# Eight blocks of a feed-forward layer in three rounded products, their low halves from an accumulating DMA

## The reference, cut to what matters

```python
h = _rmsnorm(x, norm_g[layer, 1]) * (1.0 + scale_f) + shift_f
x = x + gate_f * (jnp.square(jax.nn.relu(h @ w_fc1[layer])) @ w_fc2[layer])
```

## Time and profile before

| | |
|---|---|
| runs | 1172.93, 1177.98, 1179.79 us; median 1177.98 |
| the profiled execution | span 1171.0 us from its first to its last instruction; its time with what lies around the span is not given apart, and the runs lie 1.9 to 8.8 us above the span |
| busy share of the span | PE 95%, PEld 85%, DVE 70%, ACT 48%, POOL 4% |
| chain of work that ended last | PE 78%, DVE 10%, DMA 5%, ACT 5% |
| `fc2_0` in the trace | 306.7 to 443.3 us |
| granted clock of PE over the span | 0.985 of full speed |

### The profile page before, as it was taken

One profiled execution on the slowest core, in us unless ns is written; L12 is line 12 of the kernel. 1 busy time (PEld: TensorE's weight loads), 2 busy tenths in 40 slices (PEclk: granted clock), 3 DMA queues, 4 the chain that ended last, 5 costly groups with the idle time before them and its releaser, 6 DMA issues.

```text
span 1171.0 us, 22089 instructions
## 1 busy us (share of the span) xinstructions
PE 1112.6 (95%) x9466; PEld 995.9 (85%) x9466; DVE 816.0 (70%) x1390; ACT 557.7 (48%) x876; POOL 44.6 (4%) x71
## 2 busy tenths in 40 slices
PE   6899898999999997879999999999999999999998
PEld 4778686988888885469999999999988899988898
DVE  1599466877578674875666654478899966659955
ACT  3224633445111124554555543356568846467944
POOL 0010001000000000000000000000000000042000
PEclk8999999999999998999999999989989999999999
DMA  9887688899848957865355555525433345343342
GB/s 369 356 280 269 250 323 315 305 339 328 335 182 258 342 186 165 323 245 184 140 184 182 183 189 185 187 81 180 145 109 114 130 153 177 131 153 117 108 145 72
DMA packets 38290, 246.46 MB, mean 210 GB/s; under 512 B 4400, under 2 KB 5584, under 8 KB 9648
## 3 DMA queue, kind: packets, MB, share of 16 engines
q1 hardware_dynamic: 29072, 182.36, 45.7%
q0 software_dynamic: 6240, 43.94, 10.0%
q10 hardware_dynamic: 2880, 18.74, 3.9%
HBM read 225.24 MB, written 19.79 MB: 209 GB/s over the span
## 4 chain that ended last, share of the span: by engine, by line
PE 78%; DVE 10%; DMA 5%; ACT 5%; issue 2%; SPq 0%; ACTq 0%; DVEq 0%
PE ps L1452 16%; PE ps L1454 15%; PE ps L1456 15%; PE ps L1459 10%; PE ps L1555 4%; DMA ca_dram<-more 2%; PE ps L1648 1%; PE ps L1528 1%; PE ps L2083 1%; PE ps L1601 1%; PE ps L1539 1%; PE ps L1534 1%; DMA more<-in_ada_w 1%; DVE ring_rounded L2229 1%; DMA ada_more<-in_ada_w 1%
## 5 line engine op out<-in xcount | busy, mean ns | idle before, releaser
L1452 PE MATMUL ps<-sq_rounded,w_high_rounded 128*128 128x256 f32 x1184 | 341.6, 288 | 2.5 <-DVE mixT_rounded L2236 1.3
L1456 PE MATMUL ps<-sq_rounded,ring_rounded 128*128 128x256 f32 x1184 | 336.2, 284 | 0.0
L2229 DVE TENSOR_TENSOR ring_rounded<-ring,w_high_rounded 128x1024 fp32r<-128x1024 f32 x220 | 260.6, 1226 | 92.1 <-ACT w_high_rounded L844 91.8
L1454 PE MATMUL ps<-hT_rounded,w_high_rounded 128*128 128x256 f32 x992 | 282.1, 284 | 0.0
L844 ACT ACTIVATE w_high_rounded<-ring 128x1024 fp32r<-128x1024 f32 x220 | 219.8, 1049 | 67.0 <-PE ps L1456 66.3
L1452 PEld LDWEIGHTS ps<-sq_rounded,w_high_rounded 128*128 128x128 f32 x1184 | 228.5, 193 | 11.0 <-issue 6.7
L1456 PEld LDWEIGHTS ps<-sq_rounded,ring_rounded 128*128 128x128 f32 x1184 | 228.6, 193 | 0.0
L1454 PEld LDWEIGHTS ps<-hT_rounded,w_high_rounded 128*128 128x128 f32 x992 | 191.8, 193 | 0.1
L1452 PE MATMUL ps<-more_rounded,w_high_rounded 128*128 128x256 f32 x448 | 127.4, 284 | 0.4 <-issue 0.3
L1456 PE MATMUL ps<-more_rounded,ring_rounded 128*128 128x256 f32 x448 | 126.8, 283 | 0.0
L1459 PE MATMUL ps<-big,ring 128*128 128x256 f32 x544 | 121.0, 381 | 0.0
(11 more groups left out here) (426 smaller groups left out, 1640.3 us busy)
## 6 DMA issues: line engine op xcount, KB each, us to landing
ring<-in_blocks SPq DMA_DIRECT2D x139, 1024.0 KB, 4.9
ada_w<-in_ada_w POOLq DMA_DIRECT2D x27, 1024.0 KB, 7.7
ada_more<-in_ada_w POOLq DMA_DIRECT2D x13, 1024.0 KB, 7.6
we_dram<-we_t ACTq DMA_DIRECT2D x8, 1024.0 KB, 8.3
ca_dram<-more ACTq DMA_DIRECT2D x8, 1024.0 KB, 11.9
ring<-we_dram SPq DMA_DIRECT2D x8, 1024.0 KB, 5.5
ring<-ca_dram SPq DMA_DIRECT2D x8, 1024.0 KB, 6.8
big<-in_ada_w SPq DMA_DIRECT2D x4, 1024.0 KB, 10.9
```

The lines of the kernel that those rows point to most:

```text
L1452: nc.tensor.matmul(out, high[:, k, columns], x_high, start=start, stop=False, skip_group_check=True)
L1454: nc.tensor.matmul(out, high[:, k, columns], x_low, start=False, stop=False, skip_group_check=True)
L1456: last = nc.tensor.matmul(out, low[:, k, columns], x_high, start=False, stop=stop, skip_group_check=True)
L2229: nc.vector.tensor_tensor(rounded(w), w, w_high[:, c % 2, ks], ALU.subtract)\
```

## The change

Blocks k = 0 and 1 of each unit of `fc2_0`, eight of the 16, become split blocks. Blocks k = 2 and 3 stay plain. In the first unit the plain ones go first (order 2, 3, 0, 1), in the other units the split ones go first. In the order of the phase, blocks 0 and 1 are plain, 2 to 5 split, 6 and 7 plain, 8 and 9 split, 10 and 11 plain, 12 and 13 split, 14 and 15 plain.

The low half of these blocks' weights is made by no engine: ACT writes the high half to `w_high` and the negated rounded block over the block in the ring, and POOL then issues a DMA that reads the block from memory a second time and adds it onto the ring's slot. PE waits for that DMA once at the start of the block. ACT rounds the activations `hid` 0 to 15 into `sq` and `hT`, DVE makes their low parts in place, both before anything else of the phase on these two queues. The roundings of blocks are put between ACT's copies and stores. Since `w_high` is now in use, `near` 0 and 1 are loaded later, by ACT instead of SP, after its third square of the norm. Some semaphores are merged.

```diff
-    phase("fc2_0", [("fc2_0", k, n) for n in range(4) for k in range(4)])
+    phase("fc2_0", [("fc2_0", k, n) for n in range(4) for k in FC2_ORDER[n]])
...
+FC2_ORDER = ((2, 3, 0, 1), (0, 1, 2, 3), (0, 1, 2, 3), (0, 1, 2, 3))
+FC2_ROUND_BEHIND = {3: 4, 4: 5, 5: 6, 7: 8}
+FC2_SPLIT = tuple(4 * n + i for n in range(4) for i in range(4) if FC2_ORDER[n][i] < 2)
+LOW_BY_DMA = tuple(("fc2_0", j) for j in FC2_SPLIT)
...
+        def hid0_high(t, count):
+            return (sq if t < DT else hT)[:, t % DT:t % DT + count]
...
@@ sync
-                if b in NEAR_AT:
-                    load_near(NEAR_AT.index(b))
@@ gpsimd
+            for b in low_by_dma:
+                pool.wait_ge(w_high_ready, 2 * split_place[b] + 2)
+                pool.dma_start(rounded(ring[:, b % RING]).rearrange("p a b -> p (a b)"), dram["blocks"][laid_out[b]],
+                               accum_op=ALU.add).then_inc(w_low_dma[split_place[b] % 2], 16)
@@ scalar, round_to
+                    if b in low_by_dma:
+                        nc.scalar.activation(w_high[:, c % 2], ring[:, b % RING], ACT.Copy).then_inc(w_high_ready, 1)
+                        nc.scalar.activation(rounded(ring[:, b % RING]), ring[:, b % RING], ACT.Copy, scale=-1.0)\
+                            .then_inc(w_high_ready, 1)
...
+            def load_near(n):
+                act.wait_ge(blocks_done, first_block["fc2_0"] + FC2_SPLIT[n - 2] + 1)
+                for j in range(L):
+                    act.dma_start(s5_near[n][GC * j:GC * j + GC], ...
@@ scalar, behind the last unit of fc1_0
+            for t in range(8):
+                act.wait_ge(hid_ready, t + 1)
+                round_tiles(hid0_high(2 * t, 2), hid[:, 2 * t:2 * t + 2])
+            round_to(first_block["fc2_0"] + FC2_SPLIT[1] + 1)
             store_kernels(1)
             store_outputs(2)
             for m in range(3, 8):
...
                 copy_weights(m, (0, 1, 2, 3))
                 store_weights(m)
+                if m == 3:
+                    round_to(first_block["fc2_0"] + FC2_SPLIT[2] + 1)
                 store_kernels(m - 1)
                 store_outputs(m)
+                if m in FC2_ROUND_BEHIND:
+                    round_to(first_block["fc2_0"] + FC2_SPLIT[FC2_ROUND_BEHIND[m] - 1] + 1)
             store_kernels(7)
             act.wait_ge(k_stored, 16 * 4)
...
-            norm_stats(2, 2)
+            log_and_exp()
+            act.wait_ge(blocks_done, first_block["fc2_0"] + FC2_SPLIT[-2] + 1)
+            for p in range(3):
+                square(2, 2, p)
+            load_near(0)
+            load_near(1)
+            square(2, 2, 3)
+            norm_rstd(2)
@@ tensor, block_products
+                    if split and b in low_by_dma:
+                        if waited == 0:
+                            pe.wait_ge(w_high_ready, 2 * split_place[b] + 1)
+                            pe.wait_ge(w_low_dma[split_place[b] % 2], 16 * ((split_low[b] + 1) // 2))
+                            waited = 1
@@ vector
             s5_outputs(2)
+            for t in range(8):
+                lower_tiles("fc2_0", t, hid[:, 2 * t:2 * t + 2], hid0_high(2 * t, 2))
             gate_f = lambda k: mod(0, GATE_F, k)
```

More of the change, by code:

```diff
@@ L219, in split_plan @@
     starts = sorted((b, name) for name, b in first_block.items())
[L220 removed]
+    counts = {"vector": 0, "dma": 0}
     for i, (start, name) in enumerate(starts):
@@ L223, in split_plan @@
         for b in range(start, end) if name in SPLIT_LO else ():
-            if b - start not in {"w_in": W_IN_SPLIT, "w_out": W_OUT_SPLIT}.get(name, range(end - start)):
+            if b - start not in {"w_in": W_IN_SPLIT, "w_out": W_OUT_SPLIT, "fc2_0": FC2_SPLIT}.get(name, range(end - start)):
                 continue
@@ L229, in split_plan @@
             low[b] = counts[SPLIT_LO[name]]
-    return order, place, low
+    by_dma = [first_block[name] + j for name, j in LOW_BY_DMA]
+    return order, place, low, by_dma
 def program(nc, dram, out):
     plan, first_block = weight_plan()
-    split_order, split_place, split_low = split_plan(plan, first_block)
+    split_order, split_place, split_low, low_by_dma = split_plan(plan, first_block)
     laid_out = {b: i for i, b in enumerate(from_inputs(plan))}
-    NEAR_AT = (first_block["fc2_0"] + 10, first_block["fc2_0"] + 11)
     ctx = ExitStack()
@@ L341, in program @@
         w_low_vector = sem("w_low_vector")
+        w_low_dma = [sem(f"w_low_dma{i}") for i in range(2)]
         a_high = sem("a_high")
@@ L841, in round_to @@
                         act.wait_ge(blocks_done, split_order[c - 2] + 1 if c >= 2 else TOGETHER)
-                    for half in range(2):
+                    if b in low_by_dma:
+                        nc.scalar.activation(w_high[:, c % 2], ring[:, b % RING], ACT.Copy).then_inc(w_high_ready, 1)
+                        nc.scalar.activation(rounded(ring[:, b % RING]), ring[:, b % RING], ACT.Copy, scale=-1.0)\
+                            .then_inc(w_high_ready, 1)
+                    for half in range(2) if b not in low_by_dma else ():
                         ks = slice(4 * half, 4 * half + 4)
@@ L1443, in block_products @@
                 for k, out, columns, x, start, stop in places:
-                    if split and k // 4 == waited:
+                    if split and b in low_by_dma:
[3 more added lines that the diff above has]
+                            waited = 1
+                    elif split and k // 4 == waited:
                         pe.wait_ge(w_low_vector, 2 * split_low[b] - 1 + waited)
@@ L1500, in project_tokens, with project_deep @@
                 last.then_inc(blocks_done, 1)
-            def project_deep(phase, n, kblocks, x, arrived=None, after=None):
+            def project_deep(phase, n, kblocks, tile, arrived=None, after=None, order=range(4)):
                 ps = pair(start_unit(phase, n))
-                for kb in range(kblocks):
-                    block_products(phase, n * kblocks + kb,
+                for j, kb in enumerate(order):
+                    block_products(phase, n * kblocks + j,
                                    (lambda k: arrived(kb * KB + k)) if n == 0 and arrived else None,
-                                   [(k, ps[:, i], slice(P * i, P * i + P), at_tile(x, kb * KB + k),
-                                     kb == 0 and k == 0 and i == 0, kb == kblocks - 1 and k == KB - 1)
+                                   [(k, ps[:, i], slice(P * i, P * i + P), tile(kb * KB + k),
+                                     j == 0 and k == 0 and i == 0, j == kblocks - 1 and k == KB - 1)
                                     for k in range(KB) for i in range(2)])
                     if after:
-                        after(n * kblocks + kb)
+                        after(n * kblocks + j)
             def swept(phase, n, unit=None):
@@ L1837, in after_block, with hid_tile, hid_arrived @@
                     s5_kernels(S5_KERNEL_AT.index(16 + j))
+            def hid_tile(t):
+                if t < 2 * KB:
+                    return rounded(hid0_high(t, 1)[:, 0]), rounded(hid[:, t])
+                return hid[:, t]
+            def hid_arrived(t):
+                if t % 2:
+                    return
+                if t < 2 * KB:
+                    pe.wait_ge(a_low, SET_BASE["fc2_0"] + t // 2 + 1)
+                else:
+                    pe.wait_ge(hid_ready, t // 2 + 1)
             for n in range(4):
-                project_deep("fc2_0", n, 4, (hid,), lambda k: pe.wait_ge(hid_ready, k // 2 + 1) if k % 2 == 0 else None,
-                             after_block)
+                project_deep("fc2_0", n, 4, hid_tile, hid_arrived, after_block, FC2_ORDER[n])
             norm_stats(2)
```

43 lines of the change are left out of this document (22 added, 21 removed).

## The result

| | before | after |
|---|---|---|
| median of the runs | 1177.18 us | 1197.28 us |
| lowest to highest | 1172.93 to 1179.79 | 1188.57 to 1202.14 |
| span of the profiled execution | 1171.0 | 1196.6 |
| granted clock over the span | 0.985 | 0.970 |

The account below looks back on a forecast made before the run. PE was taken to bound the phase up to 371 us, then stores of output weights and DVE until 413.99. A 12.4 us later end plus 4 of slow clock gave +16.4: 1178 + 16 = 1194 us, range 1179 to 1217.

Parts of the forecast that it names:

- Step 1: Activations and first two split blocks: PE waits 4.8 us for the first one's DMA and starts it at 329.0.
- unknown L: Time an accumulating DMA takes to land: 11.5 us taken, between 7.7 and 15.6.
- Step 2: Third split block: rounded at 342.8, its DMA landed at 354.4, PE waiting 8.7 us from 345.7.
- Step 3: From the third split block to X: stores landing in 9 us put X at 414.3, 0.3 later than before.
- X: The moment at which DVE is done with the outputs of portion 7; 413.99 before the change.
- Step 4: From X to the phase's end: block 12 starts at 430.1, the end is 455.6 against 443.26, 12.4 us later.
- Step 5: Granted clock: it falls to its lower level behind the waits at blocks 4 and 12, 2 us each, 4 us.
- Step 6: The near loads on ACT: covered by PE's lateness; 0 taken, bounds 7 us of gain and 8 of loss.
- rivals, 1: The add lands like a plain load, L 7.7 and stores 6.7: about +2, 1180 us; chance 0.16.
- Rival 2: Slow add, L 15.6 or more, counting three times in a row: 1207 us, 1217 with slow stores; chance 0.18.
- rival 3: Faster: without the 32 near loads' hold on stores X falls to 406; with L 6, -9, 1169 us; chance 0.08.

Follow-up runs that it names:

- experiment 1: The changed kernel without its eight accumulating DMAs, so the low part of the weights is wrong: 1169.83 us, 0.9939 of the kernel before.
- experiment 2: The changed kernel with plain loads in place of the eight adding DMAs, giving wrong numbers: 1184.61 us, 1.0077 of the kernel before.
- Experiments 1 to 5: The first five follow-up kernels; the fourth only moved near 0 and 1 to ACT in the kernel before: 1181.57 us, 1.0032 of before.
- experiment 5: The changed kernel with low halves made by DVE, no negated ACT pass, last pair rounded behind portion 6: 1177.47 us, 1.0017 of the kernel before.
- experiment 3: The changed kernel with its last two split blocks rounded behind portion 6 instead of portion 7: 1192.99 us, 1.0148 of the kernel before.
- mixed version: Experiment 5 with blocks 8 and 9 given back to the adding DMA and near 2 and 3 loaded later: 1178.40 us, 1.0033 of the kernel before.

## Why the prediction was right

The forecast was 1194 in 1179 to 1217, the measurement 1197.28, and the mechanism is the one named: ACT has no lead at blocks 2, 4 and 12, PE stands there until the DMA has landed, and experiment 1 takes the whole loss away with the DMA, experiment 2 some 12 of the 20 us with the add alone. Step by step, in the time of before:

- **Step 1** held: wait 5.01 (4.8 predicted), block 2 at 329.30 (329.0). Luck helped: ACT had rounded the block 1.0 us earlier than summed, and the DMA took 1.0 longer.
- **The unknown L** was too low: 12.5 instead of 11.5. I leaned on the nearest plain load, 10.5, and gave 1.0 to the add. Both were wrong, in opposite directions: a plain load at these places takes 8.7, and experiment 2 prices the add at 3.8. Whether that is the second read no run shows.
- **Step 2** held: 8.94 (8.7).
- **Step 3 failed in its size**: X came at 421.1, not 414.3. The lag of 6.8 us is there when the store of outputs 4 is issued (370.95 for 364.2). Of it 4.9 are the slow clock of blocks 2 and 4 (2.7 + 2.2). The sum had 2 us for block 4 and none for block 2, and put them at the end, where they couldn't delay X. Another 1.2 is ACT's last copy and three issues, 2.9 us where 1.7 were taken; the store of a kernel alone held the queue for 1.63. The rest is small terms. That store of outputs 4 then landed in 6.6 us, where 9 was taken, and the lag shrank to 4.3; the next two, 9.9 and 10.2, and their issues brought it back.
- **Step 4** came out at 17.7 from X to block 12, where 15.8 were predicted: 1.0 of it is the issue of the store of outputs 7, which held ACT 1.30 us before the rounding could start, and 0.7 the landing. (The chain's "issue" of 1.75 at 426.16 is no idle time: ACT makes the high half then.)
- **Step 5** was mis-sized: 7.3 instead of 4. The clock falls behind all three long waits, and each fall costs 2.2 to 2.7.
- **Step 6** held as a net: −1.3 behind the phase for 0 predicted. Experiments 1 to 5 bear out that the lateness of PE covered the loads, as argued: with PE earlier, the part behind the phase took 2.1 to 6.5 us more than before.

ACT's rows for steps 3 and 4, in the time of after:

```profile
372.83 1.63 ACTq L1051 DMA_DIRECT2D k_dram<-more  x1
...
426.09 1.91 ACT L849 ACTIVATE w_high_rounded<-ring 128x2048 fp32r<-128x2048 f32 x1 [2.26 <-issue]
```

The sum for the phase was 16.4 and the trace has 23.3: 6.8 more to X, then 1.9, and less of the clock term at the end (2.4 for 4), which leaves 0.2. The medians show 20.1, nearer to the forecast than the trace; the profiled executions aren't the median ones on either side, so that part of the nearness is spread and no merit of the sum.

Of the rivals, 1 falls twice: L isn't 7.7, and with the plain load of experiment 2 the kernel is still slower by 0.56 to 0.98%: a landing of 8.7 is still a wait at three places, and the part behind the phase is longer. Rival 2's arithmetic, three landings in a row, is right, with L 3 us below its condition. Half of rival 3 is right too: with the DMAs gone, the kernel is 7 us faster. X falls further than the 406 it said, to 399.4, but then the last kernel (405.7) hangs on PE, and the angles on that kernel. The prediction let them hang on X alone. And only 16 of its 32 `near` loads, numbers 0 and 1, lie in the phase.

## What to carry to other kernels

A DMA that takes the place of an engine's pass moves the work off the engine and onto the path: count its landing time once at every place where the producer has no lead, and the lower clock behind every such wait. Before giving a producer more lead by moving it up in its queue, ask when its input can be there; with a ring of four slots ACT's earlier roundings mostly waited for the ring. When PE's saving is 10 us and the next limit (here DVE and ACT, 29.7 us behind the last kernel) lies 8 us away, the phase gains 8 in the end even where the low halves cost nothing.

## What the runs showed of the hardware

- An adding 1 MB DMA took 5.3 us of all 16 DMA engines where a plain load took 2.8, and POOL's issue of it 0.86 us instead of 0.53.
- Waits of PE of 5.0 to 10.9 us were each followed by the lower clock for some 5 to 6 us of work in the changed kernel; behind a 5.94 us wait and a 7.86 us one as well, there for some 3 us (first products of 0.55 us in experiment 2). Behind waits of 1.64, 1.9 and 2.5 us (after, and experiment 5) it stayed up. Behind one of 2.94 us in experiment 3 the window from 421 to 425 us ran at 0.67 of full clock, behind one of 1.88 us in the mixed version the next 4 us at 0.62. What tells these apart the runs don't show.
